# One block from the recurrence to the end of the MLP, with the output projection made ready during the last gated block

## The reference

```python
def _merge(u_four, o_hgrn, gate_pre, w_fp, w_hp, w_o, b_o):
    g_four, g_hgrn = jnp.split(jax.nn.sigmoid(gate_pre.astype(jnp.float32)).astype(u_four.dtype), N_BRANCHES, axis=-1)
    y = g_four * (_fourier_mix(u_four) @ w_fp) + g_hgrn * (o_hgrn @ w_hp)
    return y @ w_o + b_o
...
        xl = _layernorm(DEEPNORM_ALPHA * xl + mod_l[2] * mix_l, ln_post_g[l, 0], ln_post_b[l, 0])
        hl2 = _modulate(xl, mod_l[3], mod_l[4])
        xl = _layernorm(DEEPNORM_ALPHA * xl + mod_l[5] * _mlp(hl2, w_mlp1[l], b_mlp1[l], w_mlp2[l], b_mlp2[l]),
                        ln_post_g[l, 1], ln_post_b[l, 1])
```

## Time and profile before

| | us |
|---|---|
| median of 3 runs | 3272.16 (3270.93 to 3275.79) |
| the profiled execution, its own time | 3276.2 |
| its span, first to last instruction | 3274.0 |
| TensorE busy | 3098.6 (95% of the span) |
| VectorE busy | 1795.6 (55%) |
| ScalarE busy | 622.8 (19%) |
| mean granted TensorE clock | 0.979 of full speed |

### The profile page before, as it was taken

The page is one execution under the profiler, slowest core; times in us unless marked ns, Lnnn a source line. Parts: engine busy times, 40 slices in busy tenths (PEclk is TensorE's granted clock), DMA queues, the critical chain, the costliest instruction groups (busy, mean ns, idle before and its releaser), DMA issues. The chain is left out here.

```text
span 3274.0 us, 35992 instructions
## 1 busy us (share of the span) xinstructions
PE 3098.6 (95%) x14584; PEld 2553.0 (78%) x14584; DVE 1795.6 (55%) x2625; ACT 622.8 (19%) x1173; POOL 320.6 (10%) x490
## 2 busy tenths in 40 slices
PE   6999999999996899989689999999999899999997
PEld 3888888888884688868578788888888788888886
DVE  5831133121222798666388756666657556666556
ACT  2421000111112555532012211111110111111110
POOL 0322011000001222112100000000000000000000
PEclk9999999999998999989899999999999999999999
DMA  6732233333335545458545511222115212221111
GB/s 224 249 111 84 77 103 122 106 126 123 96 110 170 161 160 165 128 174 218 145 161 192 161 46 56 65 63 63 55 52 167 93 46 65 71 65 59 39 41 64
DMA packets 264569, 366.39 MB, mean 112 GB/s; under 512 B 16323, under 2 KB 180435, under 8 KB 262998
## 3 DMA queue, kind: packets, MB, share of 16 engines
q1 hardware_dynamic: 202422, 181.08, 18.2%
q0 software_dynamic: 48624, 151.56, 14.2%
q10 hardware_dynamic: 13360, 31.46, 3.0%
HBM read 257.08 MB, written 106.96 MB: 111 GB/s over the span
## 5 line engine op out<-in xcount | busy, mean ns | idle before, releaser
L144 PE MATMUL head_bank<-head_hTh,head_wh 128*128 128x512 f32 x1024 | 401.7, 392 | 3.1 <-DVE head_hTl L561 2.3
L2132 PE MATMUL tail_bank<-tail_h2h,tail_w1h 128*128 128x512 f32 x1024 | 400.3, 391 | 4.5 <-DVE tail_w1l L1901 4.5
L2150 PE MATMUL tail_bank<-tail_w2h,tail_ah 128*128 128x512 f32 x1024 | 399.7, 390 | 4.0 <-DVE tail_acc L1931 4.0
L2133 PE MATMUL tail_bank<-tail_h2l,tail_w1h 128*128 128x512 f32 x1024 | 399.9, 391 | 0.0
L2134 PE MATMUL tail_bank<-tail_h2h,tail_w1l 128*128 128x512 f32 x1024 | 399.5, 390 | 0.0
L2151 PE MATMUL tail_bank<-tail_w2l,tail_ah 128*128 128x512 f32 x1024 | 399.4, 390 | 0.0
L2152 PE MATMUL tail_bank<-tail_w2h,tail_al 128*128 128x512 f32 x1024 | 399.3, 390 | 0.0
L145 PE MATMUL head_bank<-head_hTl,head_wh 128*128 128x512 f32 x1024 | 399.2, 390 | 0.0
L146 PE MATMUL head_bank<-head_hTh,head_wl 128*128 128x512 f32 x1024 | 399.2, 390 | 0.0
L569 DVE CAST head_wh<-head_raw 128x1024 fp32r<-128x1024 f32 x64 | 44.6, 696 | 550.8 <-PE head_bank L146 416.1
L1933 DVE TENSOR_TENSOR tail_acc<-tail_acc,tail_bank 128x512 f32<-128x512 f32 x416 | 275.6, 684 | 118.6 <-PE tail_bank L2152 116.4
(11 more groups left out here) (244 smaller groups left out, 4710.6 us busy)
## 6 DMA issues: line engine op xcount, KB each, us to landing
tail_raw<-in_w SPq DMA_DIRECT2D x128, 512.0 KB, 4.0
head_raw<-in_w_in SPq DMA_DIRECT2D x64, 512.0 KB, 4.1
scratch_proj<-head_stage POOLq DMA_DIRECT2D x128, 256.0 KB, 2.7
head_x<-in_w_ada ACTq DMA_DIRECT2D x8, 2048.0 KB, 10.2
mix_gates<-scratch_proj POOLq DMA_DIRECT2D x32, 512.0 KB, 6.7
head_wa<-in_w_ada SPq DMA_DIRECT2D x8, 1024.0 KB, 9.5
mix_dec<-scratch_proj SPq DMA_DIRECT2D x32, 256.0 KB, 4.5
scratch_dft_a<-mix_fa POOLq DMA_DIRECT2D x32, 256.0 KB, 4.2
```

Source lines behind the costliest of these rows:

```text
L144: nc.tensor.matmul(out, wh, xh, start=(k == 0), stop=False)
L2132: nc.tensor.matmul(U[2 * e + c][:], w1h[:, e, k, :], hT[0][:, k, cs], start=(k == 0), stop=False)
L2133: nc.tensor.matmul(U[2 * e + c][:], w1h[:, e, k, :], hT[1][:, k, cs], start=False, stop=False)
L2150: nc.tensor.matmul(V[n % 4][:], ah[:, z, ts], w2h[:, z, cs], start=(first and z == strips[0]), stop=False)
```

## The change

`phase_tail` is gone as a block. Its five engine lists are now functions made by `tail_programs`, and each is called at the end of the same engine's list in `phase_mix`, inside one block. There is no meeting of the engines and no clearing of semaphores between the two; what protects each buffer that the projection takes over is a wait on a semaphore of the mixing part (`joined`).

The pieces of `w_out` are prepared in the last gated block: in step `m` VectorE scales piece `m` before `gated` and makes its low part after it; ScalarE rounds it, which VectorE did before. Tile 0 of `y` is loaded before the block's end and split during its steps (`low_y(0)` behind piece 4). Tile 1 is loaded after the last piece, and its split takes the place of the `wraw` buffers (`ys` 1 lies at 188 and 192 KB), so ScalarE waits for all eight low parts of the weights first.

So that this fits beside what the gating still uses, the tail's layout is new: `h2h` and `h2l` are two tiles each, `wo` is eight, `ys`, `ah`, `al`, `w2h`, `w2l` single ones, and the transfers that store and reload `h2h` and `h2l` are eight where there were four. In the mixing part `ost` and `cub` share a place, as do `of` and `mask`, and `tot` and the small vectors move into the hand-made area. SyncE therefore waits before the loads `of` 2 and 3 and `og` 0 and 1 for the masks' and the products' last use, ScalarE before the first `ost` for the first backward state, and `of` 2 and 3 are issued behind `og` 1.

```diff
+def tail_programs(nc, d, g, bx, base, bank, joined):
+    b_new, o_mm, turn_s, f_s, rms_s, gated_mm, y_s, st_y = joined
...
+    def sync(sp):
+        def load_y(j):
+            if j:
+                sp.wait_ge(yl_s, j)
+            if j in (0, 8):
+                for s in range(3):
+                    sp.wait_ge(st_y[s], 16 * len(range(s, 32 if j else 16, 3)))
...
+        sp.wait_ge(o_mm, 2 * NTILE)
+        sp.wait_ge(turn_s, NTILE)
+        for n in range(KD):
+            if n >= 2:
+                sp.wait_ge(wo_lo, n - 1)
+            sp.dma_start(wraw[:, n % 2, :], d["w_out"][n * P:(n + 1) * P, :]).then_inc(ld_w[n % 2], 16)
+            if n == 1:
+                sp.dma_start(b1[:], d["b1_col"]).then_inc(ld_r, 16)
+                sp.wait_ge(b_new, NTILE)
+                load_y(0)
+                sp.wait_ge(rms_s, NTILE)
+                sp.dma_start(rb[:], d["ln_in_b"].partition_broadcast(P)).then_inc(ld_v, 16)
+        load_y(1)
+        sp.wait_ge(gated_mm, 4 * KD)
+        load_x(0)
+        sp.dma_start(tmp[:], d["b_out"].partition_broadcast(P)).then_inc(ld_v, 16)
+        load_y(2)
...
+    def weights(dve, k):
+        dve.wait_ge(ld_w[k % 2], 16 * (k // 2 + 1))
+        nc.vector.tensor_tensor(wraw[:, k % 2, :], wraw[:, k % 2, :], g["mod2"][:], ALU.mult).then_inc(sc_s, 1)
+
+    def low_weights(dve, k):
+        dve.wait_ge(wo_hi, k + 1)
+        nc.vector.tensor_tensor(wo[k][:, 1, :], wraw[:, k % 2, :], wo[k][:, 0, :].bitcast(F32), ALU.subtract).then_inc(wo_lo, 1)
+        if k == 4:
+            low_y(dve, 0)
...
+    def scalar(act):
+        act.wait_ge(gated_mm, 3 * KD)
+        for k in range(KD):
+            act.wait_ge(sc_s, k + 1)
+            nc.scalar.copy(wo[k][:, 0, :], wraw[:, k % 2, :]).then_inc(wo_hi, 1)
+            if k == 3:
+                high_y(0)
+        act.wait_ge(wo_lo, KD)
+        high_y(1)
+        for s in range(3):
+            act.wait_ge(st_y[s], 16 * len(range(s, 32, 3)))
+        high_y(2)
...
+    def tensor(pe):
+        def free(j, c):
+            if j >= 3:
+                pe.wait_ge(rd_s, 2 * (j - 3) + c + 1)
+            else:
+                pe.wait_ge(y_s, 4 * KD - (2, 1, 0)[j])
...
 def phase_mix(nc, d, g):
...
+                else:
+                    sp.wait_ge(masked, 6 * NC)
                 sp.wait_ge(st_o[c % 2], 16 * 7)
...
-                    sp.wait_ge(masked, 6 * NC)
+                    sp.wait_ge(*climbed(NU - 1, NL))
...
+                    else:
+                        tail["weights"](dve, m)
                     gated(bi * KD + m)
+                    if bi == NB - 1:
+                        tail["low weights"](dve, m)
+            tail["vector"](dve)
...
-            for s in range(3):
-                pool.wait_ge(st_y[s], 16 * len(range(s, NB * KD, 3)))
+            tail["gpsimd"](pool)
...
-        phase_tail(nc, d, g)
```

More of the change, by code:

```diff
@@ L75, in repeat @@
         c.n = at[c] + k * (hi - lo)
[L78 to L89, removed]
 class Box:
@@ L712, in phase_mix @@
         dec, qr = place("dec", [P, 3, 2, HP], 44), place("qr", [P, 3, HP], 56)
[L713 to L717, removed]
+        kx, ks, tt = place("kx", [P, 2, 2, HP], 62), place("ks", [P, 2, HP], 70), place("tt", [P, 2 * HP], 76)
@@ L718, in phase_mix @@
+        kq, v = place("kq", [P, 4, 4, HP], 80), place("v", [P, 3, BR], 112)
+        kdT, pm, st = place("kdT", [P, 2, HP], 118), place("pm", [P, 3, HP], 122), place("st", [P, 2, HP], 128)
+        ost, cub, four = place("ost", [P, 2, HP], 132), place("cub", [P, NX, HP], 132), place("four", [P, 2, 512], 136)
+        ubr, junk = place("ubr", [P, 3, HP], 140), place("junk", [P, HP], 146)
         fa, fx, fst = place("fa", [P, 2, 2, 512], 148), place("fx", [P, 2048], 156), place("fst", [P, T], 164)
@@ L719, in phase_mix @@
         m2, m3 = place("m2", [P, 2, 2 * P], 172), place("m3", [P, 2, P], 174)
-        gates, qd, of = place("gates", [P, 3, 2, 512], 176), place("qd", [P, 2, HP], 188), place("of", [P, 2, HP], 192)
+        gates, qd, mask = place("gates", [P, 3, 2, 512], 176), place("qd", [P, 2, HP], 188), place("mask", [P, 6, P], 192, I32)
         fh, fl = ([place(f"f{x}{i}", [P, KB, 512], at + 16 * i, F32R) for i in range(2)] for x, at in (("h", 44), ("l", 52)))
-        oh, ol = ([place(f"o{x}{i}", [P, KB, 512], at + 16 * i, F32R) for i in range(2)] for x, at in (("h", 82), ("l", 90)))
@@ L724, in phase_mix @@
[L724 to L730, removed]
+        oh, ol = ([place(f"o{x}{i}", [P, KB, 512], at + 16 * i, F32R) for i in range(2)] for x, at in (("h", 80), ("l", 88)))
@@ L731, in phase_mix @@
+        wph, wpl = place("wph", [P, KB, D], 112, F32R), place("wpl", [P, KB, D], 148, F32R)
+        og, sq, ubl, of = (place(n, [P, 2, HP], at) for n, at in (("og", 76), ("sq", 128), ("ubl", 172), ("of", 192)))
+        tot = place("tot", [P, NU, 2, H], 196)
+        ms, std, rstd = (place(n, [P, 2, H], 197 + i / 8) for i, n in enumerate(("ms", "std", "rstd")))
+        ng, warm = place("ng", [P, KB], 197.5), place("warm", [P, 1], 197.625)
+        fence = bx.sb("fence", [P, 198 * 256])
         bank = bx.banks()
@@ L956, in _ @@
             load_og(1)
+            load_of(2)
+            load_of(3)
             load_four(0, 2)
@@ L979, in _ @@
                             load_back(x)
+            tail["sync"](sp)
         @block.vector
@@ L1414, in _ @@
                     from_states(bi, m)
+            tail["tensor"](pe)
         @block.scalar
@@ L1461, in output @@
                     act.wait_ge(st_o[y % 2], 16 * (y // 2))
+                else:
+                    act.wait_ge(b_new, 1)
                 nc.scalar.copy(ost[:, y % 2], OUT[:]).then_inc(o_out, 1)
@@ L1590, in _ @@
                         round_four(bi + 1, m)
+            tail["scalar"](act)
         @block.gpsimd
```

993 lines of the change are left out of this document (478 added, 515 removed).

## The result

| | us |
|---|---|
| median after | 3249.78 (3243.98 to 3252.98, 4 runs) |
| median before, all its runs | 3273.97 (3270.93 to 3278.98, 4 runs) |
| ratio, 95% interval | 0.9923 (0.9902 to 0.9943) |
| the profiled execution after, its own time | 3248.07 |
| its span | 3246.2 |

Faster, by 24.2 us between the medians. A repeat gave 0.9916 (0.9903 to 0.993), 27.5 us. Executions of one kernel lie up to 13 us apart (3269.83 to 3282.78 in 21 runs of the kernel before), so the terms are read from traces, counted from the last gated matmul.

What follows compares the result with a forecast made beforehand. TensorE bounds the kernel, so only its standstills can go: 71.34 us from last gated matmul to tile 3 becomes 5.8 + 32.64 + 2.5 = 40.9, gaining 30.4, so 3272.16 falls to 3241.8 us; range 3236 to 3250.

Steps and rivals of the forecast that it cites:

- What bounds it: Whole kernel: TensorE is busy 95% of the span, so only its standstills give time back; at the join at most 38.7 us.
- The last block's cost, 0: Last gated block: VectorE's added work makes 4.3 of 5.44 us a step, rounding and loads are hidden; cost 0.
- a landing of up to 6.5 us is free: Last gated block: weight-piece loads may take 6.5 us without delaying VectorE; about 5.5 was assumed.
- first rival: Last gated block: loads landing in 7.9 to 9.6 us make VectorE 4 to 9 us late, 3246 to 3251; chance 0.12.
- The join's chain, 5.8 us: After the last gated matmul: last gating, piece 7's low part, tile 1's rounding and low part keep TensorE standing 5.8 us.
- The clock, 2.5 us: TensorE's restart after the join's standstill: granted clock falls to 1.2 GHz, costing 2.5 us, with 0 and 3.3 as ends.
- upper end, 3.3: Restart of TensorE's clock: highest cost considered, about half of the 7.1 us from 1400.89 to 1408.00.
- Tile 2: Projection's start: tile 2's low part, behind VectorE's constants, comes at 1630, needed by 1640.1; 10 us room, 7.62 us wait goes.
- Only the block's end, 10 us: Join: something queued keeps weights out of the last block, so only some 10 us go, giving 3262; chance 0.04.
- Slower from 143 GB/s down: Last gated block: if transfers can't exceed 143 GB/s, steps take 9.2 us and all gain is lost, 3272 and up; chance 0.03.
- Time: Whole kernel: median of 3272.16 us minus 30.4 gives 3241.8; own range 3238 to 3245, chance 0.72.
- The signs: Traces: one TensorE standstill of 5 to 7 us, none before tile 2; VectorE's piece waits under 1 us, last gating unmoved.

Runs made afterwards that it cites:

- the late preparation: Changed kernel, still one block, but weight pieces loaded and split only behind the last gated step: 3276.08 us, ratio 1.0005 to the kernel before.
- 277 GB/s: Changed kernel plus an extra 512 KB copy behind each load of weight pieces 2 to 7: 3252.4 us, ratio 0.993 to the kernel before.

## Why the prediction held, and which terms were off

- **What bounds it**: that only TensorE's standstills can give time back, held. The gain stood at the join, 29.1 us where 30.4 were forecast; the runs with the layout alone and with the late preparation show that neither pays without the prepared weights.
- **The last block's cost, 0**: right for TensorE (45.00 of 45 us busy), wrong for VectorE. The failed step is "a landing of up to 6.5 us is free", with 5.5 taken: the pieces took 7.3. VectorE waited 1.84, 1.32 and 2.07 us for pieces. It made up most of it, its work being 4.3 of 5.44 us a step, but the last delay passed through the gates' issue to the last gating: 1.4 us. That is the first rival's mechanism at less than its price of 4 to 9 us, which stood for landings of 7.9 and 9.6 us and assumed that nothing is made up (reckoned in the same way, 7.3 us would give 2.2); at 277 GB/s the standstill is 5.9 us longer.
- **The join's chain, 5.8 us**: measured 7.45 = 1.65 until the gating + 1.93 + 1.25 + 1.08 + 1.54. The forecast of the same parts was 0.26 + 1.93 + 1.24 + 1.07 + 1.31. All but 0.3 of the difference is the late gates.
- **The clock, 2.5 us**: measured 1619.34 to 1654.13, 34.79, less 32.64 for the matmuls: 2.15. In the other variants of the changed kernel with a standstill, of 6 to 37 us, it is 2.0 to 2.8. The prediction's upper end, 3.3, had read the 7.11 us of the earlier trace rows as matmuls of 128x512 throughout; from 1406.15 twelve of 128x128 lie in them. The matmuls stand 0.43 us apart until 1623.7, at the level of 1.2 GHz. The Trainium skill ("TensorE: Matmul & The Clock Gate", What's actually happening) says that the throttled clock is the default and that activity releases it; this trace agrees. Where TensorE did not stand still, in the run with tile 0 first, the whole term vanished.
- **Tile 2**: its low part was forecast for 1630, 20.0 us after the end of the last gated matmul, and began at 1631.00, 19.1 us after it. TensorE wants it 21.76 + 2.15 us after 1619.34, at 1643.3, so the room was 11 us. The load of `ag` took 8.3 us instead of the 4.2 reckoned, and the room took it.
- **Only the block's end, 10 us**: the weights did not stay out of the last block, so this rival did not arise. With the late preparation the earlier start was given back whole, in the wait for tile 1; for the order of before its worth is open. With prepared weights, the meeting and the jump put back cost 6.0 us.
- **Slower from 143 GB/s down**: refuted by 234 and 277 GB/s in the same place. The rate of before was what was asked for. The Trainium skill's table ("DMA: Bandwidth & Descriptors", Bandwidth) had made the traffic fit with room, by an estimate of 3.8 us a step, and the first rival worth nothing. It fitted in bytes, but a single transfer landed in 7.3 us, and on that the wait hung.
- **Time**: 3274.0 - 30.4 had stood for the span; 3246.2 is 2.6 over it, 1.3 from the join and the rest from where the two executions stood before and behind it. The median of four, 3249.78, is 8 over the forecast, of which 1.8 come from the runs before, whose median over all four is 3273.97; that of the repeat is 3 over. The runs scatter by as much, and both ratios' intervals hold the 29.1 of the trace (0.9911). That 3249.78 still lies in the range, 0.2 us under its end of 3250, is luck. It is outside the forecast's own 3238 to 3245 and where the first rival stood, 3246 to 3251, so only the traces say that the rival cost 1.4 us and not 8.
- **The signs**: one standstill, tile 1's low part as its releaser, no wait before tile 2 and the pace of later tiles came as forecast. The standstill lay over its 5 to 7 us. VectorE's waits on pieces passed 1 us, and a wait on the gates moved the last gating, which had been named a sign of being wrong; it was one in small.
- **Left out**: the prediction did not see that the order of tiles 0 and 1 made the standstill at all. The chain of tile 1 (6.1 us) is shorter than tile 0's matmuls (10.9), which were ready to go but for piece 7, and that was done before their turn came to it.

## What to carry to other kernels

When work is prepared under another stage's matmuls, ask next which single operand the restart still waits for, and give TensorE a piece of work that doesn't need it; here that was worth another 8 us. Check a removed block end by what is next in line: it is worth nothing if the chain behind it grows by as much, and it was worth 6 us where the chain was short. Whether a transfer is hidden goes by its landing time at the new total rate, not by the bytes.

## What the runs showed of the hardware

- A meeting of the engines with a jump to the projection's lists took 6.0 us; a whole empty block, its clearing included, 0.7. Why they differ is open: no run changed the lists' length alone.
- A weight piece of 512 KB landed in 3.7 us behind the join of the kernel before, in 7.3 at 234 GB/s and in 8.3 at 277 (medians), and TensorE's gated matmuls kept their pace at both rates.
- With no standstill at the join, the granted clock stayed at 1.00 through 84 us and two stages. Behind the single standstill of the changed kernel's variants it cost 2.0 to 2.8 us, behind the two of the kernel before 1.3 and 2.5.
